# Dense stages: moving operand and PSUM output of TensorE with a step of minus one

## The chip, the cores and the metric

One core of a Trainium2 chip runs the whole kernel in one launch. The metric is device time in microseconds, median of several runs.

## The reference

Two transformer blocks are applied one after the other to 512 tokens of width 1024 (batch 1). The first has two layers and carries 256 context tokens beside the 512 latent ones: each layer has a mixer with three branches (a 2-D Fourier transform, neighbourhood attention, latent attention with rotary positions), gates and an output projection, then a SwiGLU feed-forward of hidden width 2816; the second layer drops the context at its end. The second block has one layer: sliding-window attention, a gated linear recurrence and forgetting attention side by side, an output projection, and 16 experts of width 256 with two chosen per token. All of it is float32:

```python
f, nq, nk, nv, cq, ckv, kr, g = jnp.split(h @ lp['w_in'], IN_OFFSETS, axis=-1)
...
proj = jnp.einsum('bngi,gio->bngo', y, w_branch)
gate = jax.nn.sigmoid(g.reshape(b, n, N_BRANCH, D_MODEL).astype(jnp.float32)).astype(proj.dtype)
return jnp.sum(gate * proj, axis=2) @ w_out
...
return (jax.nn.silu(h @ w_gate) * (h @ w_up)) @ w_down
```

The products with weight matrices (`w_in`, `w_branch`, `w_out`, the feed-forward, and `w_in_2`, `w_out_2` of the second block) are what the change is about.

## The kernel before

Activations stay on the chip as [128 partitions, blocks of 128 features, tokens]. Each float32 matrix product is made of three matmuls in the type fp32r: a value is split into a high half and the rest, and high x high, low weight x high and high weight x low are summed in PSUM.

`run_dense` (L1024) runs a list of layers. A layer (class `Dense`, made by `project`, `residual`, `gated_branch` and `swiglu`) is a row of chunks, each 128 output features wide. For each chunk, SyncE loads the weights into `w_raw` (L1130), ScalarE casts them to `w_hi` (L1208), VectorE subtracts to get `w_lo` (L1218), TensorE multiplies, and ScalarE or VectorE takes the result out of PSUM (for example L1254, L1281, L1429, L1440). Two of each buffer and two halves of PSUM, four banks each, alternate, so that the chunks overlap. `lo_ready`, `psum_free` and `mm_done` are the semaphores between them. Background work (adaptive modulation vectors, L944 on VectorE, L979 on TensorE) is put between chunks.

The moving operand is the activation (`hi` and `lo`, up to 768 tokens), cut by `groups` into 512 latent tokens and 256 context tokens (where there are any); the stationary operand is a 128 x 128 block of weights. The output of a group of tokens is a slice of one PSUM bank (`bank`, L1156).

TensorE has three ways through a chunk: the first two chunks behind a norm (L1169, L1170, L1175), whose inputs become ready block by block; the first chunk of a stage whose input is split while it runs (L1181, L1182, L1186); and all others (L1187 to L1194), which go through one group of tokens after the other. Per group, all blocks get high x high and low x high (L1191, L1192), then all blocks get high x low (L1194), all into the same output. All three ways walk the tokens upwards.

Parts that the change leaves alone and that the prediction reads: the Fourier stage's L1560, whose stationary operand takes every second token, and L1575; the attention's plain float32 products L2180 and L2185; the eviction L1254 of `project`, which for some layers writes in another order (`by_tile`, `by_column`); the experts' products (L3264 to L3291), which have their own loop.

```python
def by_tile(o, s):
    return o.rearrange("p (t r w) -> p r t w", t=4, r=ROWS), s.rearrange("p (r t w) -> p r t w", t=4, r=ROWS)

def by_column(o, s):
    return o.rearrange("p (w r) -> p r w", r=ROWS), s.rearrange("p (r w) -> p r w", r=ROWS)
```

Of the kernel before, what the change touches and what calls it, by code (L numbers as in the profile page):

```python
# [108 lines left out]
def groups(T):  # L109

    return [(0, min(T, LAT))] + ([(LAT, T - LAT)] if T > LAT else [])


def program(nc, g, out):

    root = ExitStack()
    with root:
# [906 lines left out]
        def run_dense(ring, layers, pool_program=None, background=(), norm=None, presplit=False, lead=None, raw_first=None):  # L1024

            raw, whi, wlo = ring
# [7 lines left out]
            def enter(d):  # L1034

                for t, v in d.start.items():
                    t.base = v
                return d
# [6 lines left out]
            def behind(who, eng, n):  # L1045
                for b in background:
                    b.run(who, eng, n)
                if who == "act" and isinstance(norm, Norm):
                    norm.act_later(eng, n)
# [39 lines left out]
            def rest(who, eng):  # L1089
                for b in background:  # L1090
                    for n in range(len(pieces), b.end):
                        b.run(who, eng, n)

            with ExitStack() as c:
                block = c.enter_context(nc.Block())

                if pool_program is not None or isinstance(norm, GroupNorm):
                    @block.gpsimd
                    def _(pool):
                        def low_half(pool, n):  # L1100
                            d = enter(pieces[n][0])
                            pool.wait_ge(hi_ready[n].sem, hi_ready[n].base + 1)
                            pool.tensor_tensor(wlo[:, n, 0:d.blocks, :], raw[:, n, 0:d.blocks, :], whi[:, n, 0:d.blocks, :].bitcast(F32),
                                               ALU.subtract).then_inc(lo_ready[n].sem, 1)

                        if isinstance(norm, GroupNorm):
                            norm.pool(pool)
                        elif norm is not None and norm.running:
                            norm.pool(pool, low_half)
                        if lead is not None:  # L1110
                            lead.pool_program(pool)
                        if pool_program is not None:
                            pool_program(pool)
# [22 lines left out]
                @block.tensor  # L1136
                def _(pe):
                    d0 = None
                    if norm is not None:
                        norm.pe(pe)  # L1140
                    if lead is not None:
                        lead.pe_program(pe)
                    for n, (d, i, jj) in enumerate(pieces):
                        enter(d)
                        if d is not d0:
                            d0 = d
                            if "pe" in d.before:
                                d.before["pe"](pe)
                        behind("pe", pe, n)
                        if lead is not None and n == 1:  # L1150
                            lead.evicted(pe)
                        j = jj % 2
                        pe.wait_ge(lo_ready[j].sem, d.use(i, jj) + (lo_ready[j].base + 1))
                        pe.wait_ge(psum_free[j].sem, d.use(i, jj) + psum_free[j].base)
                        for part, (off, b0, nb, hi, lo) in enumerate(d.parts):
                            def bank(t0, tn):  # L1156
                                return ps[:, 4 * BANK * j + off + t0:4 * BANK * j + off + t0 + tn]

                            if norm is not None and n < 2:
                                if n == 0:  # L1160
                                    for b in range(nb):
                                        norm.first_high(pe, b)
                                        for n1 in range(2):
                                            if b == 0:
                                                pe.wait_ge(lo_ready[n1].sem, d.use(0, n1) + (lo_ready[n1].base + 1))
                                                pe.wait_ge(psum_free[n1].sem, d.use(0, n1) + psum_free[n1].base)
                                            for t0, tn in groups(d.T):
                                                o = ps[:, 4 * BANK * n1 + off + t0:4 * BANK * n1 + off + t0 + tn]
                                                pe.matmul(o, whi[:, n1, b0 + b, :], hi[:, b, t0:t0 + tn], start=(b == 0), stop=False, skip_group_check=True)  # L1169
                                                pe.matmul(o, wlo[:, n1, b0 + b, :], hi[:, b, t0:t0 + tn], start=False, stop=False, skip_group_check=True)  # L1170
                                for b in range(nb):
                                    if n == 0:
                                        norm.first_use(pe, b)
                                    for t0, tn in groups(d.T):
                                        m = pe.matmul(bank(t0, tn), whi[:, j, b0 + b, :], lo[:, b, t0:t0 + tn], start=False, stop=(b == nb - 1), skip_group_check=True)  # L1175
                            elif d.needs and (i, jj) == (0, 0) and part == len(d.parts) - 1:
                                hi_done, lo_done = d.needs
                                for b in range(nb):
                                    pe.wait_ge(hi_done.sem, hi_done.base + b + 1)
                                    for t0, tn in groups(d.T):  # L1180
                                        pe.matmul(bank(t0, tn), whi[:, j, b0 + b, :], hi[:, b, t0:t0 + tn], start=(b == 0), stop=False, skip_group_check=True)  # L1181
                                        pe.matmul(bank(t0, tn), wlo[:, j, b0 + b, :], hi[:, b, t0:t0 + tn], start=False, stop=False, skip_group_check=True)  # L1182
                                for b in range(nb):
                                    pe.wait_ge(lo_done.sem, lo_done.base + b + 1)
                                    for t0, tn in groups(d.T):
                                        m = pe.matmul(bank(t0, tn), whi[:, j, b0 + b, :], lo[:, b, t0:t0 + tn], start=False, stop=(b == nb - 1), skip_group_check=True)  # L1186
                            else:  # L1187
                                for t0, tn in groups(d.T):
                                    o = bank(t0, tn)
                                    for b in range(nb):  # L1190
                                        pe.matmul(o, whi[:, j, b0 + b, :], hi[:, b, t0:t0 + tn], start=(b == 0), stop=False)  # L1191
                                        pe.matmul(o, wlo[:, j, b0 + b, :], hi[:, b, t0:t0 + tn], start=False, stop=False)  # L1192
                                    for b in range(nb):
                                        m = pe.matmul(o, whi[:, j, b0 + b, :], lo[:, b, t0:t0 + tn], start=False, stop=(b == nb - 1))  # L1194
                            if part == 0 and d.part_done is not None:
                                m.then_inc(d.part_done.sem, 1)
                        m.then_inc(mm_done[j].sem, 1)
                    rest("pe", pe)
# [2292 lines left out]
```

## Time and profile before

| | |
|---|---|
| median of 3 runs | 3154.04 us (3150.85 to 3156.76) |
| the profiled execution | 3151.03 us |
| its span, first to last instruction | 3149.2 us |
| mean granted TensorE clock | 0.958 of full |
| instructions | 37052 |

Busy times are of the profiled execution. A matmul's duration runs from its start to the modelled end of its last column and overlaps the next matmul, so the pace of a stream is the distance between starts: the length of a run of n equal matmuls, less one duration, by n - 1. Idle time before a group is the time that its engine waited for it.

### The profile page before, as it was taken

To read this page: it belongs to the slowest core of one execution; us is meant where nothing else is said; L and a number is where in the kernel's file an instruction comes from. 1 tells how busy PE (TensorE), PEld (TensorE's weight loads), DVE (VectorE), ACT (ScalarE), POOL (GpSimd) and SP (SyncE) were. 2 spreads that over 40 slices of the span, in tenths; PEclk is the share of its full clock that TensorE was granted. 3 is DMA by queue.
4 is the path that set the end of the run, shared out by engine and by line. 5 is a ranking of instruction groups with operands and counts; after the bars stand their busy time and mean duration, and the time that the engine had idled before them with its cause. 6 is when DMAs were issued, how large, how long until landed. Compare 5 with 4: busy or idle time off the path is not lost. (4 is left out here: it accounts for less than half of the span.)

```text
span 3149.2 us, 37052 instructions
## 1 busy us (share of the span) xinstructions
PE 2893.3 (92%) x14705; PEld 2306.7 (73%) x14705; DVE 1686.4 (54%) x2379; ACT 1209.5 (38%) x1800; POOL 453.8 (14%) x445
## 2 busy tenths in 40 slices
PE   7998899999979999999799799998999978876995
PEld 4886566888868888888587457886888846555774
DVE  3385665233355666642515563446656454655997
ACT  5324555122243211221534443324323244635774
POOL 4400200000040000002500100002000124122332
PEclk9999899999989999999899899999999989897997
DMA  7650101222113444431620103333656326335962
GB/s 213 131 167 19 25 1 51 61 61 66 52 51 104 142 126 134 140 96 33 109 65 16 25 11 91 100 85 110 191 172 190 110 39 83 155 90 187 377 237 81
DMA packets 397871, 330.11 MB, mean 105 GB/s; under 512 B 38038, under 2 KB 340484, under 8 KB 397572
## 3 DMA queue, kind: packets, MB, share of 16 engines
q1 hardware_dynamic: 384196, 304.56, 33.1%
q0 software_dynamic: 13248, 23.13, 3.1%
q8 instruction: 117, 1.92, 0.2%
q14 instruction: 54, 0.44, 0.0%
q10 hardware_dynamic: 256, 0.07, 0.0%
HBM read 331.96 MB, written 30.33 MB: 115 GB/s over the span
## 5 line engine op out<-in xcount | busy, mean ns | idle before, releaser
L1191 PE MATMUL ps<-ahi,w_hi 128*128 128x512 f32 (+1 forms) x2264 | 766.4, 352 | 5.2 <-DVE w_lo L1218 5.2
L1192 PE MATMUL ps<-ahi,w_lo 128*128 128x512 f32 (+1 forms) x2264 | 766.1, 352 | 0.0
L1218 DVE TENSOR_TENSOR w_lo<-w_raw,w_hi 128x1024 fp32r<-128x1024 f32 (+2 forms) x242 | 340.6, 1409 | 365.6 <-ACT w_hi L1208 363.5
L1191 PEld LDWEIGHTS ps<-ahi,w_hi 128*128 128x128 f32 x2264 | 428.0, 189 | 69.0 <-DVE w_lo L1218 7.5
L1194 PE MATMUL ps<-alo,w_hi 128*128 128x512 f32 (+1 forms) x2264 | 472.9, 351 | 0.0
L1192 PEld LDWEIGHTS ps<-ahi,w_lo 128*128 128x128 f32 x2264 | 428.4, 189 | 59.2 <-issue 0.2
L1208 ACT CAST w_hi<-w_raw 128x1024 fp32r<-128x1024 f32 (+2 forms) x244 | 285.6, 1171 | 461.6 <-PE ps L1194 366.7
L1194 PEld LDWEIGHTS ps<-alo,w_hi 128*128 128x128 f32 x2264 | 377.6, 189 | 56.7
L944 DVE SCALAR_TENSOR_TENSOR vec_acc<-vec_w,csilu,vec_acc 128x512 f32<-128x512 f32 x364 | 255.2, 747 | 8.3 <-DVE vec_acc L944 5.5
L1358 POOL TENSOR_TENSOR xsum<-x 128x768 f32<-128x768 f32 (+1 forms) x4 | 6.3, 1567 | 1407.0 <-DVE x L1337 1407.0
L1281 DVE SCALAR_TENSOR_TENSOR x<-ps,mod,x 128x512 f32<-128x512 f32 x80 | 51.4, 668 | 232.3 <-PE ps L1194 219.3
L1191 PE MATMUL ps<-hhi,w_hi 128*128 128x512 f32 (+1 forms) x462 | 158.2, 355 | 0.0
L1192 PE MATMUL ps<-hhi,w_lo 128*128 128x512 f32 (+1 forms) x462 | 157.6, 354 | 0.0
L3318 ACT CAST e_hi<-e_raw 128x2048 fp32r<-128x2048 f32 x69 | 131.7, 1913 | 29.3 <-DMA e_raw<-in_w_up 16.2
L1432 ACT CAST hhi<-hf 128x768 fp32r<-128x768 f32 (+1 forms) x44 | 32.0, 728 | 265.8 <-DVE hf L1440 265.8
L1515 DVE TENSOR_TENSOR gp<-sg,ps 128x768 f32<-128x768 f32 (+1 forms) x32 | 26.2, 820 | 196.7 <-PE ps L1194 179.6
L1506 ACT ACTIVATE sg<-ps 128x768 f32<-128x768 f32 (+1 forms) x48 | 33.8, 705 | 240.9 <-PE ps L1194 240.9
L1254 ACT COPY proj<-ps 128x512 f32<-128x512 f32 (+2 forms) x58 | 40.1, 759 | 177.9 <-PE ps L1194 166.1
L2180 PE MATMUL ps<-mla_pt,proj 128*128 128x512 f32 x192 | 102.5, 616 | 0.0
L1879 POOL TENSOR_SCALAR prob<-prob,nm 128x512 f32<-128x512 f32 (+3 forms) x64 | 37.6, 587 | 414.4 <-DVE nm L1804 414.4
L1191 PEld LDWEIGHTS ps<-hhi,w_hi 128*128 128x128 f32 x462 | 87.3, 189 | 13.0 <-issue 0.2
L1192 PEld LDWEIGHTS ps<-hhi,w_lo 128*128 128x128 f32 x462 | 87.4, 189 | 12.6 <-issue 0.2
(556 smaller groups left out, 5231.6 us busy)
## 6 DMA issues: line engine op xcount, KB each, us to landing
vec_w<-in_w_mod SPq DMA_DIRECT2D x128, 512.0 KB, 4.0
w_raw<-in_w_in SPq DMA_DIRECT2D x102, 512.0 KB, 3.9
e_raw<-in_w_gate SPq DMA_DIRECT2D x46, 512.0 KB
e_raw<-in_w_up SPq DMA_DIRECT2D x46, 512.0 KB
e_raw<-in_w_down SPq DMA_DIRECT2D x46, 512.0 KB
w_raw<-in_w_ffn_gate SPq DMA_DIRECT2D x44, 512.0 KB, 4.4
w_raw<-in_w_ffn_up SPq DMA_DIRECT2D x44, 512.0 KB, 3.7
w_raw<-in_w_ffn_down SPq DMA_DIRECT2D x32, 704.0 KB, 4.4
```

Source lines behind the costliest of these rows:

```text
L944: m = dve.scalar_tensor_tensor(out=acc, in0=w, scalar=f, in1=acc, op0=ALU.mult, op1=ALU.add)
L1191: pe.matmul(o, whi[:, j, b0 + b, :], hi[:, b, t0:t0 + tn], start=(b == 0), stop=False)
L1192: pe.matmul(o, wlo[:, j, b0 + b, :], hi[:, b, t0:t0 + tn], start=False, stop=False)
L1194: m = pe.matmul(o, whi[:, j, b0 + b, :], lo[:, b, t0:t0 + tn], start=False, stop=(b == nb - 1))
L1208: act.copy(whi[:, j, 0:d.blocks, :], raw_of(d, i, jj)).then_inc(hi_ready[j].sem, 1)
L1218: dve.tensor_tensor(wlo[:, j, 0:d.blocks, :], raw_of(d, i, jj), whi[:, j, 0:d.blocks, :].bitcast(F32), ALU.subtract).then_inc(lo_ready[j]. ...
L1254: m = act.copy(o_, s_) if scale is None else act.activation(o_, s_, ACT.Identity, scale=scale)
L1281: m = dve.scalar_tensor_tensor(out=xo, in0=ps[:, b + t0:b + t0 + tn], scalar=mod[:, v, bass.ds(i * 2 + (gate + jj), 1)], in1=xo, op0=ALU.m ...
L1506: act.activation(sg[:, jj, :], ps[:, 4 * BANK * jj:4 * BANK * jj + T], ACT.Sigmoid).then_inc(gated.sem, 1)
L1879: pool.tensor_scalar(self.prob[:, j, slot, 0:u.keys], self.prob[:, j, slot, 0:u.keys], self.nm[:, j, slot, 3:4], 1.0, ALU.mult, ALU.mult). ...
L2180: m = pe.matmul(ps[:, bank:bank + LAT], weight(b, j), self.pt[:, s % 3, :], start=(b == 0), stop=(b == kt - 1))
L3318: act.copy(whi[:, n % HI, :], raw[:, n % RAW, :]).then_inc(e_hi.sem, 1)
```

## The change

In the third way through a chunk, the output slice is taken with a step of minus one, and so is each moving operand. The first column that enters the array is that of the last token of the group, and it goes to the last place of the slice. Stationary operands, order of the matmuls, semaphores and the two other ways stay.

```diff
                             else:
+
                                 for t0, tn in groups(d.T):
-                                    o = bank(t0, tn)
+                                    o = bank(t0, tn)[:, ::-1]
                                     for b in range(nb):
-                                        pe.matmul(o, whi[:, j, b0 + b, :], hi[:, b, t0:t0 + tn], start=(b == 0), stop=False)
-                                        pe.matmul(o, wlo[:, j, b0 + b, :], hi[:, b, t0:t0 + tn], start=False, stop=False)
+                                        high = hi[:, b, t0:t0 + tn][:, ::-1]
+                                        pe.matmul(o, whi[:, j, b0 + b, :], high, start=(b == 0), stop=False)
+                                        pe.matmul(o, wlo[:, j, b0 + b, :], high, start=False, stop=False)
                                     for b in range(nb):
-                                        m = pe.matmul(o, whi[:, j, b0 + b, :], lo[:, b, t0:t0 + tn], start=False, stop=(b == nb - 1))
+                                        m = pe.matmul(o, whi[:, j, b0 + b, :], lo[:, b, t0:t0 + tn][:, ::-1], start=False, stop=(b == nb - 1))
```

## Rows read from the trace of the kernel before

**Rows 1.** The page: busy us, share of the span and instructions of each engine

```profile
PE 2893.3 (92%) x14705; PEld 2306.7 (73%) x14705; DVE 1686.4 (54%) x2379; ACT 1209.5 (38%) x1800; POOL 453.8 (14%) x445
```

**Rows 2.** The page: busy tenths in 40 equal slices of the span

```profile
PE   7998899999979999999799799998999978876995
...
PEclk9999899999989999999899899999999989897997
```

**Rows 3.** Busy time per stretch; columns as the second line names them

```profile
core 0: us, PE busy (x) PEld busy (x) DVE busy (x) ACT busy (x) POOL busy (x), PEclk, DMA share, GB/s
...
80.00:250.00 170.00, 164.35 (x915) 141.35 (x914) 93.29 (x126) 53.58 (x67) 31.96 (x40) 0.97 0.57 143
...
540.00:1130.00 590.00, 573.18 (x3234) 499.53 (x3233) 258.39 (x286) 157.74 (x178) 33.54 (x17) 0.99 0.29 82
...
1200.00:1400.00 200.00, 200.00 (x1148) 174.70 (x1147) 123.10 (x157) 45.14 (x50) 0.00 (x0) 1.00 0.42 127
...
1920.00:2540.00 620.00, 605.90 (x2631) 492.19 (x2629) 315.87 (x371) 191.96 (x239) 44.11 (x31) 0.99 0.44 130
```

**Rows 4.** Waits of TensorE's matmuls: us in total, times, longest us

```profile
PE ps L1191 <- DVE w_lo L1218: 16.9, 8, 10.0
```

**Rows 5.** Timeline of TensorE, 1300 to 1306 us: start, length, instructions

```profile
1299.81 1.30 PE L1194 MATMUL ps<-alo,w_hi 128*128 128x512 f32 x5
...
1302.86 1.12 PE L1194 MATMUL ps<-alo,w_hi 128*128 128x256 f32 x8
```

**Rows 6.** Groups of L1191 by form: count, busy us, mean ns, idle before

```profile
L1191 PE MATMUL ps<-ahi,w_hi 128*128 128x512 f32 x1456 | 568.9, 391 | 5.2 <-DVE w_lo L1218 5.2
...
L1191 PE MATMUL ps<-ahi,w_hi 128*128 128x256 f32 x808 | 197.5, 282 | 0.0
L1191 PE MATMUL ps<-hhi,w_hi 128*128 128x512 f32 x308 | 120.7, 392 | 0.0
...
L1191 PE MATMUL ps<-a2hi,w_hi 128*128 128x512 f32 x160 | 66.7, 417 | 11.7 <-DVE w_lo L1218 11.7
...
L1191 PE MATMUL ps<-yhi,w_hi 128*128 128x512 f32 x168 | 65.6, 390 | 0.0
...
L1191 PE MATMUL ps<-hhi,w_hi 128*128 128x256 f32 x154 | 37.5, 283 | 0.0
...
L1191 PE MATMUL ps<-yhi,w_hi 128*128 128x256 f32 x84 | 20.9, 282 | 0.0
```

**Rows 7.** Weight loads of L1560 and L1575: ns min/median/max

```profile
L1560 PEld LDWEIGHTS ps<-dft_chan,proj x80: 195/197/198, 252.2 to 1684.8; 128*128 128x128 f32 x80
...
L1575 PEld LDWEIGHTS ps<-dft_seq,dft_u x160: 186/190/192, 255.6 to 1691.7; 128*128 128x128 f32 x160
```

**Rows 8.** Plain float32 matmuls: timeline at 1798 and 433 us, durations of L2180

```profile
1798.78 1.02 PE L2180 MATMUL ps<-mla_pt,proj 128*128 128x512 f32 x2
...
433.28 1.89 PE L2185 MATMUL ps<-mla_pt,proj 128*128 128x256 f32 x8
...
L2180 PE MATMUL ps<-mla_pt,proj x192: 590/592/1061, 402.7 to 1903.9; 128*128 128x512 f32 x192
...
L2185 PE MATMUL ps<-mla_pt,proj 128*128 128x256 f32 x32 | 7.6, 381 | 1.3 <-ACT mla_pt L2226 1.3
```

**Rows 9.** ScalarE's L1254, 80 to 250 us: `by_column` (COPY), `by_tile` (ACTIVATE)

```profile
L1254 ACT COPY proj<-ps 128x512 f32<-128x512 f32 x8 | 9.7, 1210 | 45.5 <-PE ps L1194 45.5
...
L1254 ACT ACTIVATE proj<-ps 128x512 f32<-128x512 f32 x4 | 2.4, 598 | 22.5 <-PE ps L1194 22.5
```

**Rows 10.** Groups by form: L1194 in the changed loop, the experts' L3266

```profile
L1194 PE MATMUL ps<-alo,w_hi 128*128 128x512 f32 x1456 | 359.6, 389 | 0.0
...
L1194 PE MATMUL ps<-alo,w_hi 128*128 128x256 f32 x808 | 113.3, 283 | 0.0
...
L3266 PE MATMUL ps<-a2lo,a2hi 128*128 128x512 f32 x92 | 36.1, 392 | 0.0
```

## The prediction

> **What bounds the kernel now.** I read the page's busy table first, then its strip of 40 slices, then the busy time per stretch, then the waits of TensorE, and last the timeline inside one dense stage.
>
> The busy table gives TensorE 2893.3 us of 3149.2 (92%), VectorE 54%, ScalarE 38% [rows 1]. In the strip the matmul row stands at 7 to 9 tenths nearly everywhere and the granted clock at 9 tenths but for eight slices with 7 or 8 [rows 2]. By stretch: over the first dense stage (80 to 250 us) matmuls fill 164.35 of 170 us, over 540 to 1130 us 573.18 of 590, over 1920 to 2540 us 605.90 of 620; from 1200 to 1400 us they fill 200.00 of 200.00 us at a granted clock of 1.00, the 2.4 GHz level [rows 3]. The waits agree: in the whole run the first matmul of the changed loop (L1191) waits 16.9 us for anybody [rows 4]. So the dense stages run at the pace at which TensorE takes columns. DMA share is 0.42 and VectorE 62% in that full stretch [rows 3]: nothing else is near its end there, and no other engine has slack to lend to a slower matmul.
>
> The timeline gives the pace. A run of five 512-column matmuls of L1194 lasts 1.30 us; less the 0.389 us of the last one, that is 4 steps of 0.228 us. Eight of 256 columns last 1.12 us: 7 steps of (1.12 - 0.283)/7 = 0.1196 us [rows 5]. The difference, 0.108 us for 256 columns, is 0.423 ns a column; about 12 ns a matmul is not columns. This is the only quantity that the change can touch.
>
> **What the change touches.** Only the loop at L1187 to L1194, which every chunk takes except the first two behind a norm (L1169 to L1175) and the first of a stage with streamed inputs (L1181 to L1186). It adds and removes no instruction, wait, DMA or byte, and moves no step past a queue. `hi`, `lo` and the bank are walked from the last token to the first, all three together, so column t still lands at t, and ScalarE and VectorE read the bank as before, after the same semaphore. The weights are loaded in the old order. So each part has one answer, apart from the price of a matmul.
>
> How many matmuls: L1191 has 1456 + 308 + 168 + 160 = 2092 of 512 columns and 808 + 154 + 84 = 1046 of 256 [rows 6]; L1192 and L1194 have as many each. Together 6276 and 3138. At today's steps they take 6276 x 0.228 + 3138 x 0.1196 = 1431 + 375 = 1806 us, 57% of the span. None of it is covered by anything, so every nanosecond that a 512-column matmul gains or loses is 6.3 us of the kernel, and on a 256-column one 3.1 us.
>
> **The price of a descending step.** No instruction of the kernel before walks backwards, so I bound it.
>
> *Below.* A matmul step has 12 ns that are not columns; were they all to vanish, the gain would be 9414 x 12 ns = 113 us. I exclude it: the first column of a matmul follows the last of the one before in the same manner whichever end they start from, since all three of a block run in the same direction into the same bank. Nothing about the order makes a column cheaper than 0.423 ns, the pace of the engine's upper clock level. So the lower end is zero.
>
> *Above, near.* The mildest uneven walk in the trace is the stationary operand of L1560, which takes every second element (`first:first + 2 * P - 1:2`): its load takes 197 ns in the median against 190 ns for that of L1575, which takes neighbours [rows 7]. That is 7 ns for 128 elements. By the same measure the moving operand would pay 28 ns for 512 and 14 ns for 256: 6276 x 0.028 + 3138 x 0.014 = 176 + 44 = 220 us.
>
> *Above, middle.* TensorE taking columns at half its pace would look like its plain float32 matmuls, which run at half the column pace under the same clock: two of L2180 last 1.02 us, which less 0.592 us for the last is a step of 0.43 us, and eight of L2185 last 1.89 us, (1.89 - 0.38)/7 = 0.216 us for 256 columns [rows 8]. Against the changed loop's steps that is +0.202 and +0.096 us: 6276 x 0.202 + 3138 x 0.096 = 1268 + 301 = 1569 us.
>
> *Above, far.* ScalarE's eviction L1254 shows what a scattered walk costs. In the order `by_column` each element lands 8 elements from the last one, and 512 of them take 1210 ns; in the order `by_tile`, which goes in runs of 16 neighbours and then jumps, 598 ns [rows 9]. The scattered walk costs (1210 - 598)/512 = 1.2 ns an element. For 6276 x 512 + 3138 x 256 = 4.02 million columns that is 4820 us.
>
> *Which I take.* What these three rows have in common is distance: neighbours, and runs of neighbours with a jump now and then, are free; a step of two elements costs 4%; a step of 8 costs double. A step of minus one is a walk among neighbours, and the row that it is nearest to is the run of 16 with its jumps, at nothing. I take zero. What no row shows is direction, and that is why the upper ends stay in the range or among the rivals.
>
> The Trainium skill, page "Advanced Engine Details and Errata", sections "SBUF Cachelines" and "PSUM Cachelines", makes the same thing a matter of lines: successive accesses inside one 16-byte line of SBUF are at full rate, and PSUM works in lines of two float32 values. By that reading, a descending walk over an even count from an aligned start meets the same lines with the same number of hits, and costs nothing; the ScalarE rows agree with it (32-byte steps cost double), and for TensorE's moving operand and output no row of this trace shows it. The same section also says that any non-contiguous access pattern slows matmuls significantly; if minus one counts as that, the rule speaks against this change, and what it would do is the second rival.
>
> **Sum.** 0 us on the profiled execution: 3151.0 us, span 3149.2. The median of the three runs is 3154.04, 3 us above it, and they spread from 3150.85 to 3156.76; the forecast is 3154. A measurement of this kernel can tell about 0.2% (6.3 us) from no change.
>
> **Rivals.**
>
> *The walk backwards halves the column pace (0.16), slower.* Place: each of the 9414 matmuls, in the fetch of the moving operand or in the write to PSUM; one is enough, as the slower side sets the pace. For it: a step of 0.423 ns a column means two 4-byte values per tick of the lower 1.2 GHz level on both sides, so something takes columns in pairs, and pairs may be formed upwards only; the plain float32 rows show that a one-at-a-time pace exists. Against it: a pair of neighbours is the same pair from either end. It decides as soon as a 512-column step rises by more than 1 ns, since 6276 ns is the 0.2%. Price: 3151 + 1569 = 4720 us, less at most the 17 us that L1191 waits today. In the Trainium skill this is the PSUM rule named above.
>
> *A small cost on each matmul (0.08), slower.* An address unit that restarts, or a pair that straddles, priced by the step of two: up to 3151 + 220 = 3371 us. For it: the 7 ns are real. Against it: the weight load is another path than either that changes, and minus one is nearer than two.
>
> *Scattered price (0.02), slower:* 3151 + 4820, about 7970 us. Only if each column opened its own access; `by_tile` speaks against.
>
> *The change does not do what it says (0.02 of the main case).* If the patterns were turned back into ascending ones on the way to the chip, everything would be as before: 3154 us. It can't be told from the forecast by time.
>
> **How the numbers follow.** Main case 0.74 with the last rival in it, time within the spread of the runs; of this 0.03 falls on the fast side of 0.2%, 0.70 within, 0.01 on the slow side, for an interval on medians of three that spread by 0.19% themselves. Add 0.08 + 0.16 + 0.02 for slower: faster 0.03, same 0.70, slower 0.27. The range takes in the main case and the small cost, 0.82: from 3145 (3151 less the 0.2%) to 3375 (3371 and the runs' spread). Half pace and scattered price, 0.18 together, are left out; between 3375 and 4700 I have no mechanism. The main case's own range is 3145 to 3162.
>
> **What the profile after would show.** If right: steps of 0.228 and 0.120 us inside the timeline of a dense stage, 389 and 283 ns in the groups of L1194's line, piece after piece at the same time from the start, busy 200 of 200 us still. If half pace: durations near 592 and 380 ns in the changed line, and unchanged ones of 390 in the two loops that stay ascending and in the experts (L3266 at 392 [rows 10]); ScalarE and VectorE at a third of the span. If the small cost: steps of 0.23 to 0.256 us with everything else alike. The ascending loops beside the descending one are the control. I am wrong if the changed line's 512-column step moves by over 1 ns while theirs does not.

## The result and the profile after

The changed kernel takes 3183.85 us (3182.46 to 3186.52, 4 runs) beside 3155.40 us of the kernel before in the same comparison: ratio 1.0099, 95% interval 1.0087 to 1.0112. It is slower by 0.9 to 1.1%. The two medians are 28.5 us apart, and single executions of one kernel spread by 4 to 6 us. Its profiled execution took 3184.81 us with a span of 3183.0, which is 33.8 us more than the execution that the prediction was summed against.

The page's busy table, the stretch from 1200 to 1400 us (columns as in [rows 3]) and the first matmul's wait, after the change:

```profile
PE 2929.3 (92%) x14705; PEld 2306.6 (72%) x14705; DVE 1686.3 (53%) x2379; ACT 1207.4 (38%) x1800; POOL 448.2 (14%) x445
```

```profile
1200.00:1400.00 200.00, 200.00 (x1128) 171.53 (x1127) 127.73 (x165) 44.12 (x50) 0.00 (x0) 1.00 0.43 129
```

```profile
PE ps L1193 <- DVE w_lo L1220: 16.0, 8, 9.3
```

TensorE's busy time rose by 36 us, as much as the span within 3 us, and every other engine's stayed within 6 us [rows 1]. In the full stretch the engine is as full as before and at the same clock, but it gets through 1128 matmuls where it was 1148 [rows 3]. Its wait is what it was [rows 4]. So nothing waits longer; the matmuls themselves take longer. The timeline of the first dense stage gives the steps, first before, then after the change (the changed lines are L1193, L1194 and L1196 now):

```profile
96.29 1.98 PE L1194 MATMUL ps<-alo,w_hi 128*128 128x512 f32 x8
```

```profile
96.58 2.03 PE L1196 MATMUL ps<-alo,w_hi 128*128 128x512 f32 x8
100.34 1.11 PE L1196 MATMUL ps<-alo,w_hi 128*128 128x256 f32 x8
```

The groups by form, with the experts' line, which the change leaves alone:

```profile
L1196 PE MATMUL ps<-alo,w_hi 128*128 128x512 f32 x1456 | 369.6, 397 | 0.0
...
L1196 PE MATMUL ps<-alo,w_hi 128*128 128x256 f32 x808 | 112.2, 282 | 0.0
...
L3268 PE MATMUL ps<-a2lo,a2hi 128*128 128x512 f32 x92 | 36.1, 392 | 0.0
```

A step of 512 columns is (2.03 - 0.397)/7 = 0.2333 us; before, a run of eight lasted 1.98 us, (1.98 - 0.389)/7 = 0.2273. A step of 256 is (1.11 - 0.282)/7 = 0.1183 us, before 0.1196 [rows 5]. So 6276 matmuls lost 6.0 ns each and 3138 won 1.3 ns: +37.7 - 4.1 = +33.6 us, which is the 33.8 us of the span. These are single runs of eight; over all neighbouring matmuls of the three lines in the two traces (steps with a wait in them left out) the mean steps are 227.4 and 233.3 ns for 512 columns, 119.7 and 118.4 for 256, nearly the same differences. The experts' matmul stays at 392 ns [rows 10]. The ascending loop L1186, the control that the prediction named, stays at a median of 389 ns before and after, where the changed line went from 389 to 397: the sign by which it said that it would be wrong. Where the time went is thus settled by the trace; why a backward walk costs 6 ns on 512 columns and gains 1 ns on 256 is not.

### The profile page after: what moved, and what is told of

It reads as the page before. It is cut to its first block and busy times, and to the rows that moved or that the text cites. A ratio compares the mean times of both kernels' runs of the same rounds, so it can differ in the third digit from the quotient of the medians.

```text
span 3183.0 us, 37052 instructions
## 1 busy us (share of the span) xinstructions
PE 2929.3 (92%) x14705; PEld 2306.6 (72%) x14705; DVE 1686.3 (53%) x2379; ACT 1207.4 (38%) x1800; POOL 448.2 (14%) x445
## 5 line engine op out<-in xcount | busy, mean ns | idle before, releaser
L1193 PE MATMUL ps<-ahi,w_hi 128*128 128x512 f32 (+1 forms) x2264 | 775.4, 356 | 5.1 <-DVE w_lo L1220 5.1
L1194 PE MATMUL ps<-ahi,w_lo 128*128 128x512 f32 (+1 forms) x2264 | 774.7, 357 | 0.0
L1193 PEld LDWEIGHTS ps<-ahi,w_hi 128*128 128x128 f32 x2264 | 426.1, 188 | 76.9 <-DVE w_lo L1220 7.4
L1196 PE MATMUL ps<-alo,w_hi 128*128 128x512 f32 (+1 forms) x2264 | 481.7, 356 | 0.0
L1194 PEld LDWEIGHTS ps<-ahi,w_lo 128*128 128x128 f32 x2264 | 425.5, 188 | 66.9 <-issue 0.2
L1196 PEld LDWEIGHTS ps<-alo,w_hi 128*128 128x128 f32 x2264 | 376.4, 188 | 66.0
L1193 PE MATMUL ps<-hhi,w_hi 128*128 128x512 f32 (+1 forms) x462 | 160.2, 360 | 0.0
L1194 PE MATMUL ps<-hhi,w_lo 128*128 128x512 f32 (+1 forms) x462 | 159.5, 359 | 0.0
L1508 ACT ACTIVATE sg<-ps 128x768 f32<-128x768 f32 (+1 forms) x48 | 33.8, 704 | 247.4 <-PE ps L1196 247.4
L1193 PEld LDWEIGHTS ps<-hhi,w_hi 128*128 128x128 f32 x462 | 86.9, 188 | 14.8 <-issue 0.2
L1431 ACT ACTIVATE sg<-ps 128x768 f32<-128x768 f32 (+1 forms) x44 | 31.0, 704 | 174.9 <-PE ps L1196 174.3
L1194 PEld LDWEIGHTS ps<-hhi,w_lo 128*128 128x128 f32 x462 | 86.8, 188 | 14.3 <-issue 0.2
```

Source lines behind the costliest of these rows:

```text
L1193: pe.matmul(o, whi[:, j, b0 + b, :], high, start=(b == 0), stop=False)
L1194: pe.matmul(o, wlo[:, j, b0 + b, :], high, start=False, stop=False)
L1196: m = pe.matmul(o, whi[:, j, b0 + b, :], lo[:, b, t0:t0 + tn][:, ::-1], start=False, stop=(b == nb - 1))
L1508: act.activation(sg[:, jj, :], ps[:, 4 * BANK * jj:4 * BANK * jj + T], ACT.Sigmoid).then_inc(gated.sem, 1)
```

## The experiments

**Which of the two walks.** In the first run only the moving operand is taken backwards, in the second only the output:

```diff
-                                    o = bank(t0, tn)[:, ::-1]
+                                    o = bank(t0, tn)
```

```diff
-                                        high = hi[:, b, t0:t0 + tn][:, ::-1]
+                                        high = hi[:, b, t0:t0 + tn]
...
-                                        m = pe.matmul(o, whi[:, j, b0 + b, :], lo[:, b, t0:t0 + tn][:, ::-1], start=False, stop=(b == nb - 1))
+                                        m = pe.matmul(o, whi[:, j, b0 + b, :], lo[:, b, t0:t0 + tn], start=False, stop=(b == nb - 1))
```

> Only the moving operand walks backwards, the output upwards; so the token order of each dense output is turned round, the amount of work is the same. Read theory (the fetch of the moving operand from SBUF is what costs): the whole slowdown is here, a 512-column step of 233 ns against 227, and 3184 us, +0.9 to 1.1% on the kernel before. Write theory (the PSUM output is what costs): 227 ns and 3155 us. If both walks pay a share: between, about 230 ns and 3170 us.

> Only the PSUM output walks backwards, the moving operand upwards; token order of each dense output is turned round. Read theory: 227 ns per 512-column step and 3155 us. Write theory: 233 ns and 3184 us. A third theory, that a matched pair of directions matters: both this run and its mirror would be slower than the one with both backwards, over 3184 us.

Moving operand backwards: 3184.57 us, ratio 1.0105 (1.0086 to 1.0125). Output backwards: 3151.49 us, ratio 0.9999 (0.9989 to 1.0008). The same two runs of eight in the timelines, first of the former kernel, then of the latter:

```profile
97.31 2.03 PE L1196 MATMUL ps<-alo,w_hi 128*128 128x512 f32 x8
...
101.07 1.11 PE L1196 MATMUL ps<-alo,w_hi 128*128 128x256 f32 x8
```

```profile
96.55 1.98 PE L1196 MATMUL ps<-alo,w_hi 128*128 128x512 f32 x8
100.28 1.12 PE L1196 MATMUL ps<-alo,w_hi 128*128 128x256 f32 x8
```

All of the cost is in the fetch of the moving operand from SBUF. Writing PSUM backwards is free, and a mixed pair of directions costs no more than a matched one. The Trainium skill, page "PSUM — Partial Sum Buffer", section "Specifications (TRN2)", says that any non-contiguous access pattern slows matmuls significantly; here a step of minus one in the output does not count as one, with 227 ns a step and the ratio above.

**Which group of tokens.** The two walks backwards for one length of group only:

```diff
-                                    o = bank(t0, tn)[:, ::-1]
+                                    way = -1 if tn == LAT else 1
+                                    o = bank(t0, tn)[:, ::way]
```

(and `[:, ::way]` on `hi` and `lo`; the other kernel has 1 and -1 exchanged).

> Both walks backwards in groups of 512 tokens alone, the 256-token groups upwards. By the steps of the two traces the 512-column matmuls lose 6.3 ns each (6276 of them, 39 us) and the 256-column ones win 1 to 2 ns each (3138 of them, 4 us): this should be slower than the changed kernel by about 4 us, 3188 us, +1.1%. If instead the cost sat at the change from one group to the other, it would be a good deal more or less than that.

> Both walks backwards in the 256-token groups alone. If prices add up group by group (512 groups at 227 ns as before, 256 groups 1 to 2 ns less on 3138 matmuls), this is 3 to 4 us faster than the kernel before, -0.1%, at the edge of what can be told; only_512 and this one then add up to the changed kernel.

Only the 512-token groups: 3189.36 us against 3152.09, ratio 1.0121 (1.0102 to 1.0140), +37.3 us where the steps give +37.7. Only the 256-token groups: 3147.02 us against 3151.33, ratio 0.9981 (0.9972 to 0.9991), -4.3 us where the steps give -4.1. They add up to +33.0. So the prices of the two sizes add up, whatever the other group does. The second of the two is faster than the kernel before by 0.2%, which is about as small as can be told here. Its timeline:

```profile
93.61 1.11 PE L1197 MATMUL ps<-alo,w_hi 128*128 128x256 f32 x8
98.18 1.98 PE L1197 MATMUL ps<-alo,w_hi 128*128 128x512 f32 x8
```

**The price by itself.** A small kernel that only runs rows of 16 equal matmuls, one source line for each form, after a warm-up of 64. This kernel and the two that follow were each run once:

```python
for r in R: pe.matmul(o(1, 0, 512, 1), wt(r), m(0, 512, 1), start=(r == 0), stop=(r == 15), ...)
```

where the last argument of `o` and `m` turns the output and the moving operand round, and the first of `m` is the element at which it starts.

> A kernel that leaves the reference's work out and runs rows of 16 matmuls with a warm clock, one source line per form: 128 to 512 columns, moving and output forwards or backwards, other start addresses, other banks, bfloat16 and plain float32. Read or write theory, if the price is per column: 6.3 ns at 512 columns, 3.1 at 256, 1.6 at 128, and only in the rows where the guilty walk is backwards. If it is a price per matmul: 6 ns at each size where weight loads do not bound. If it comes from how the walk meets another one (weights loaded from SBUF, the next matmul's first write): it changes with start address or with the bank. A fetch in pairs or lines of bytes would give bfloat16 another price than fp32r, and plain float32, at half the column pace, none.

Timeline of TensorE in it: start, length. L67 both forwards, L68 both backwards, L69 moving operand alone, L70 output alone, all fp32r; L96 bfloat16 both backwards, L97 moving alone; L103 plain float32 forwards, L104 backwards.

```profile
32.91 3.79 PE L67 MATMUL ps<-x,w 128*128 128x512 f32 x16
36.53 3.90 PE L68 MATMUL ps<-x,w 128*128 128x512 f32 x16
40.27 3.90 PE L69 MATMUL ps<-x,w 128*128 128x512 f32 x16
44.00 3.81 PE L70 MATMUL ps<-x,w 128*128 128x512 f32 x16
...
106.78 3.62 PE L96 MATMUL ps<-xh,wh 128*128 128x512 bf16 x16
110.23 3.62 PE L97 MATMUL ps<-xh,wh 128*128 128x512 bf16 x16
113.69 3.62 PE L98 MATMUL ps<-xh,wh 128*128 128x512 bf16 x15
...
124.13 13.90 PE L103 MATMUL ps<-raw_x,raw_w 128*128 128x512 f32 x32
137.87 13.90 PE L104 MATMUL ps<-raw_x,raw_w 128*128 128x512 f32 x32
151.61 13.90 PE L105 MATMUL ps<-raw_x,raw_w 128*128 128x512 f32 x32
```

From one line's start to the next there are 16 steps: fp32r forwards (36.53 - 32.91)/16 = 0.226 us, both backwards 0.234, moving alone 0.233. bfloat16 takes 0.216 us backwards, in L96 and L97, and as much forwards (L95), and plain float32 (137.87 - 124.13)/32 = 0.429 in each direction. So of the three types, at these starts, only fp32r minds. bfloat16 stands 2.6 ns above 512 columns at 2.4 GHz (213.3 ns); fp32r stands 13 ns above them forwards and 20 ns backwards. So the change added to a surcharge that fp32r pays anyway. Whether that surcharge lies between the matmuls or is spread along their columns, these rows don't tell.

By size the price is neither of the two that were expected. L71 to L73 have 448 columns (forwards, both backwards, moving alone), L83 to L85 the same with 256:

```profile
47.65 3.40 PE L71 MATMUL ps<-x,w 128*128 128x448 f32 x16
50.89 3.47 PE L72 MATMUL ps<-x,w 128*128 128x448 f32 x16
54.20 3.47 PE L73 MATMUL ps<-x,w 128*128 128x448 f32 x16
...
81.44 2.08 PE L83 MATMUL ps<-x,w 128*128 128x256 f32 x16
83.35 2.06 PE L84 MATMUL ps<-x,w 128*128 128x256 f32 x16
85.25 2.06 PE L85 MATMUL ps<-x,w 128*128 128x256 f32 x16
```

Backwards costs 7 ns at 512 columns, 4 at 448 (202.5 and 206.9 ns a step), 2 at 384, 1 at 320, and gains 1 at 256 (119.4 and 118.8). That falls much faster than the columns do, and it is not one price per matmul either. Taking four banks in turn changes nothing: the steps of 512 columns are 227 ns forwards (the median of L111) and 234 backwards (L112).

The same kernel held the hint for what follows. Forwards, 512 columns, moving operand started 2 elements further (L115) and 256 elements further (L119):

```profile
217.93 3.90 PE L115 MATMUL ps<-x,w 128*128 128x512 f32 x16
...
232.88 3.79 PE L119 MATMUL ps<-x,w 128*128 128x512 f32 x16
```

That is 0.233 us a step, (221.66 - 217.93)/16 with the start of the next line, L116, for a walk upwards that merely starts elsewhere, and (3.79 - 0.392)/15 = 0.227 again at 256 elements. **My theory of a price of walking backwards no longer stood alone**: the rival was that the kernel before stands at a good place, and that the backward walk has none.

**Weights or activations.** The next small kernel cut the stationary operand to fewer columns and moved the starts of both.

> A kernel without the reference's work: rows of 16 fp32r matmuls, 512 or 256 columns, both directions, with the stationary operand cut to 96, 64 and 32 columns, with it moved by 2 to 64 elements, and with the moving operand moved by 2 to 128. Theory A (the weight load that runs beside a matmul and the stream of the moving operand meet in SBUF, and direction only changes how they meet): with fewer weight columns the step of 512 columns falls from 227 and 233 ns towards the 216 ns that bfloat16 shows, in both directions; and moving the weights changes the step as moving the activations does (233 and 230 ns at +2 and +4 elements forwards), with some phase where the backward walk is as fast as the forward one. Theory B (walking backwards itself is slower, 6 ns on 512 columns): the difference stays with 32 weight columns and at every phase.

L67 and L68 have 128 weight columns, forwards and backwards, L73 and L74 have 32:

```profile
32.42 3.79 PE L67 MATMUL ps<-x,w 128*128 128x512 f32 x16
36.05 3.90 PE L68 MATMUL ps<-x,w 128*128 128x512 f32 x16
...
54.63 3.86 PE L73 MATMUL ps<-x,w 128*32 128x512 f32 x16
58.33 3.90 PE L74 MATMUL ps<-x,w 128*32 128x512 f32 x16
```

This missed in part. Fewer weight columns did not bring the step down to 216 ns: with 32 it is (3.86 - 0.39)/15 = 0.231 forwards and 0.234 backwards, and with 96 and 64 it is 0.231 and 0.230 forwards. Less to load thus made the forward step 3 to 4 ns longer and left the backward one as it was. So the surcharge does not grow with the length of the weight load. (With 256 columns the forward step fell instead, from 119.5 ns to 114 to 117.) But moving the weights alone, by 16 elements, did bring a forward step from 227 to 234 ns. Moving the activations alone by 16 gave 230, by 2 to 12 elements 232 to 234. So the place of the weights matters as that of the activations does, though not with the same value for the same shift. No phase gave a backward step under 233 ns.

**The grid.** 11 starts of the moving operand by 11 of the weights (0 to 56 elements), both directions.

> A kernel without the reference's work: rows of 16 fp32r matmuls, 512 columns, both directions, in a grid of 11 starts of the moving operand by 11 starts of the weights (0 to 56 elements), then a smaller grid of 256 columns, then other orders of the weight blocks. Address theory: forwards, cells where both are moved by the same amount are as fast as the one with neither moved (227 ns), the others go up to 234; backwards there are cells at 227 too. Direction theory: backwards no cell lies under 233 ns, whatever the phase.

Some of its cells. Forwards, moving operand and weights both at 40 (L163) and both at 48 (L175), moving at 48 and weights at 0 (L166); backwards, moving 48 and weights 0 (L287), both at 48 (L296):

```profile
387.80 3.80 PE L163 MATMUL ps<-x,w 128*128 128x512 f32 x16
398.89 3.89 PE L166 MATMUL ps<-x,w 128*128 128x512 f32 x16
432.41 3.80 PE L175 MATMUL ps<-x,w 128*128 128x512 f32 x16
...
850.98 3.90 PE L287 MATMUL ps<-x,w 128*128 128x512 f32 x16
884.58 3.90 PE L296 MATMUL ps<-x,w 128*128 128x512 f32 x16
```

Forwards, 8 of the 11 cells with equal starts have a mean step between 226.7 and 228.9 ns, and 9 of the 110 others; the mean of those others is 232.3. Backwards all 121 cells lie between 233.1 and 236.7 ns, and none has the good value. So both theories hold a half: the forward price depends on where the two operands lie, and backwards each place that was tried costs what a bad place costs. The difference of the two starts does not decide alone: both at 4 or both at 12 are slow (232.8 ns), 4 and 8 or 8 and 12 are fast (226.7).

Two things limit this reading. All 121 backward walks have 512 columns and an even start, so each begins on an odd element; a backward walk from an even element, or an upward one from an odd element, was not run, and a good place for the backward walk is not excluded there. And what ran just before leaves its mark: with one weight block for all 16 matmuls a forward row has a mean step of 230.3 ns in the second small kernel and 228.3 in this one, and in both its last steps are 227. Eight orders of the weight blocks other than the usual one, the single block among them, all have 228.2 to 228.3 forwards and 233.5 to 233.6 backwards, so the order of the blocks is not the cause. The smaller grid of 256 columns has 116.7 to 119.5 ns forwards and 117.8 to 120.0 backwards; one of its cells (weights 16 elements on) has 117.5 here and 113.7 in the second small kernel, so at 256 columns the two starts alone do not fix the step.

**In the kernel itself.** The ring of weight buffers moved by 64 bytes (16 elements), in the kernel before and in the changed one, and then in the kernel before the activations `ahi`, `alo` (and all behind them) as well, and likewise `a2hi` and `a2lo` of the second block. `place(c, n)` starts the ring n bytes behind a multiple of 256 bytes:

```diff
-            place(c, 0)
+            place(c, 64)
```

```diff
+            c.enter_context(nc.sbuf_tensor("gap64_a", [P, 16], F32))
             ahi = sb(c, "ahi", [P, KT, ALL], F32R)
```

> The kernel before, all walks upwards, with the ring of weight buffers 64 bytes (16 elements) further on in SBUF and nothing else. Address theory (what a 512-column fp32r matmul pays over 216 ns depends on where its moving operand and its weights lie to each other, and the kernel before stands at the best place, which the backward walk has not): by the row of the second small kernel, 234.1 ns against 226.7 on 6276 matmuls and 113.7 against 119.5 on 3138, +46 - 18 = +28 us, 3180 us, as slow as the changed kernel though nothing walks backwards. Direction theory (an upward walk costs 227 ns wherever it lies, a backward one 233): 3152 us.

> The changed kernel, all dense walks backwards, with the same 64 bytes. By the same rows the backward walk hardly minds: 233.6 ns against 233.5 and 117.9 against 118.9, -3 us, 3181 us. If address theory holds and the backward walk has a good place of its own that 64 bytes lead to, it falls to 227 ns and 3150 us.

> The kernel before, all walks upwards, with the weight ring 64 bytes further on as in the run before, and now the activations (both halves of the input to the dense stages) 64 bytes further on too. If what counts is how the two lie to each other, everything is as in the kernel before: 227 and 120 ns, 3154 us. If what counts is where each lies by itself, it stays at 233 ns for 512 columns and 3172 us or more.

Kernel before with the ring moved: 3171.91 us, ratio 1.0060 (1.0043 to 1.0077), with nothing walking backwards. Its timeline, in the first dense stage and in a stage whose moving operand is `ylo`:

```profile
95.98 2.03 PE L1194 MATMUL ps<-alo,w_hi 128*128 128x512 f32 x8
99.66 1.07 PE L1194 MATMUL ps<-alo,w_hi 128*128 128x256 f32 x8
...
564.70 1.07 PE L1194 MATMUL ps<-ylo,w_hi 128*128 128x512 f32 x4
```

`yhi` and `ylo` lie behind the ring in SBUF and so moved with it: their step stayed at (1.07 - 0.389)/3 = 0.227 us, while `ahi` and `alo`, which did not move, went to (2.03 - 0.395)/7 = 0.2336, and their 256 columns to (1.07 - 0.277)/7 = 0.1133. By steps, over the matmuls that don't read `y` (504 and 252 of the 6276 and 3138 do): 5772 x 6.3 - 2886 x 6.3 = +36.4 - 18.2 = +18 us; measured 3171.91 - 3154.02 = +17.9. The close agreement is in part luck: these are single runs of eight, and by the mean steps over the whole trace (233.3 and 114.8 ns against 227.4 and 119.7) the sum is +20 us, still inside the interval of the ratio. The expected 28 us had counted the `y` stages in and taken 7.4 ns for the 512 columns.

Changed kernel with the ring moved: 3182.76 us against 3154.02, ratio 1.0090 (1.0073 to 1.0107), as without it, its steps as those of the changed kernel:

```profile
93.02 1.11 PE L1196 MATMUL ps<-alo,w_hi 128*128 128x256 f32 x8
97.70 2.03 PE L1196 MATMUL ps<-alo,w_hi 128*128 128x512 f32 x8
```

Ring and activations moved together: 3154.59 us, ratio 1.0010 (0.9999 to 1.0022), and the steps of the kernel before are back:

```profile
95.92 1.98 PE L1194 MATMUL ps<-alo,w_hi 128*128 128x512 f32 x8
99.64 1.12 PE L1194 MATMUL ps<-alo,w_hi 128*128 128x256 f32 x8
```

Moving the activations alone was not tried in this kernel.

## Why the prediction was wrong

*What bounds the kernel, and that nothing covers the matmuls*: right. The stretch from 1200 to 1400 us is full before and after, and per-matmul nanoseconds came out one for one: +33.6 us by steps, 33.8 by spans.

*The counts*, 6276 and 3138: right; the changed kernel and the runs with one group length each add up by them.

*"I take zero"*: this step failed. It measured +6.0 ns on 512 columns and -1.3 ns on 256. I had asked which row of the trace a step of minus one is nearest to, and taken ScalarE's walk in runs of 16 [rows 9]: another engine, another port, and a walk whose direction is up. I let distance stand for direction. And I overlooked that the trace of the kernel before shows TensorE's fetch in a second arrangement. The latent attention's fp32r matmuls, all upwards and at a granted clock of 1.00, have 512 columns too (on 96 partitions):

```profile
435.25 0.40 PE L2116 MATMUL ps<-mla_qhi,mla_klo 96*128 96x512 f32 x1
435.49 0.40 PE L2117 MATMUL ps<-mla_qlo,mla_khi 96*128 96x512 f32 x1
435.73 0.52 PE L2133 MATMUL ps<-mla_khi,mla_qhi 96*128 96x512 f32 x2
```

Their steps are 0.24 us, over the whole trace 235 ns in the mean from L2116 to L2117, where the changed loop has 227. That was the sign that a 512-column fp32r step is not one number. The Trainium skill, page "Advanced Engine Details and Errata", section "SBUF Cachelines", from which I drew the same, does not give these 6 ns: a descending walk touches the same 16-byte lines as often.

*"The first column of a matmul follows the last of the one before in the same manner whichever end they start from"*, the reason for which I excluded that the 12 ns beside the columns could change: wrong too as a reason: what a matmul pays beside its columns did change. Where in the matmul it lies, no run shows. With the chip's own rows one sees 2.6 ns in bfloat16, 13 ns in fp32r forwards at a good place, 20 ns in fp32r backwards or at a bad place. I had treated a surcharge as a constant of the engine when it was a property of this type and these addresses.

*The small-cost rival* had the right sign, kind and order of size, and the range reached over it. Its price of 28 and 14 ns (220 us) was taken from a weight load with a step of two [rows 7]; measured were 6.0 and -1.3 ns, 33.6 us. Its two mechanisms, a restart and a straddling pair, are not needed for such a price, since an upward walk at another even address pays the same; for the backward walk itself no run excludes them. *Half pace* and *scattered price* fell: no step of the changed loop is near 0.43 us. The row that priced half pace was misread as well: a 0.43 us step is one of two records of a plain float32 matmul (last section), so such a matmul goes at a quarter of the column pace, not at half.

*The chances*: 0.70 for no change rested on one argument with no row of its own engine behind it. A surcharge of 12 ns that the trace showed and that I could not explain, on 9414 uncovered matmuls, was the reason to give the small cost more. That the range reached over the result is owed to the borrowed price, not to a mechanism that came true.

What stays open is the mechanism inside SBUF: how the fetch of an fp32r moving operand meets the weights' reads so that most equal starts are good, why fewer weight columns make a forward step of 512 columns longer, and why 256 columns can gain where 512 lose. The Trainium skill, page "TensorE: Matmul & The Clock Gate", section "Part 2: What happens when you issue a matmul", says that loading the next weights does not steal read bandwidth from the running matmul. For fp32r the rows here show that the weights' reads do not leave the running matmul alone: moving nothing but the weights against the activations by 64 bytes cost 6 ns on each 512-column matmul, and the measurement decides. Whether it is bandwidth or the order of requests, no run here tells.

## What to carry to other kernels

Where TensorE is full, read the step between matmul starts against columns over clock, and treat what is left over as something that can move: in fp32r it depends on where the moving operand and the weights start, and 64 bytes were worth 0.6% of this kernel. Before a change of layout, allocation or direction, compare that step for each size of matmul, since the sizes can move in opposite directions. Walking PSUM backwards was free here; walking a 512-column fp32r moving operand backwards gave up the good place, while bfloat16 and plain float32 did not mind at the one start that was tried.

## What the runs showed of the hardware that was not expected

- The step of an fp32r matmul of 512 columns, upwards, is 227 to 229 ns at 17 of 121 pairs of starts and 229.5 to 235.3 at the others; bfloat16 has 216 ns in both directions, at the one start that was tried.
- Backwards, 121 arrangements gave 233.1 to 236.7 ns; those whose moving operand started 2 elements on gave 235.5 to 235.6 throughout.
- 256 columns are fast where 512 are slow: in the kernel with the weights 64 bytes on they have a mean step of 114.8 ns (113 in the run shown), where 512 columns have 233; in the kernel before 120 and 227. The small kernels gave two values for one such pair of starts, so what else decides stays open.
- 16 plain float32 matmuls leave 32 records of 0.429 us each. The step that I had read as half pace in [rows 8] is thus one of two records of a matmul, and a plain float32 matmul takes 0.86 us for 512 columns.
